# The first norm's modulations on TensorE: a block of two transformers on one Trainium2 core

## What is computed

```python
sh1, sc1, gt1, sh2, sc2, gt2 = [m[:, None, :] for m in adaln_params(c, w_mod[l], b_mod[l])]
csh1, csc1, cgt1, csh2, csc2, cgt2 = adaln_params(c_ctx, w_mod[l], b_mod[l])
pc = project(modulate(ctx, norm1_g[l], csh1, csc1), w_in[l])
...
px = project(modulate(x, norm1_g[l], sh1, sc1), w_in[l])
```

## Time and profile before

| | us |
|---|---|
| median of 3 runs | 1780.99 |
| the profiled execution | 1781.36 |
| its span, first to last instruction | 1779.5 |
| PE busy | 1590.7 (89%) |
| DVE busy | 968.7 (54%) |
| ACT busy | 720.5 (40%) |
| POOL busy | 206.1 (12%) |
| mean granted clock of PE | 0.942 |

### The profile page before, as it was taken

How to read it: one execution, slowest core, us unless ns; L and a number is a source line. 1 busy time by engine, 2 the same in 40 slices (tenths; PEclk the granted TensorE clock), 3 DMA queues, 4 the chain that set the end, 5 groups by cost and what they waited for, 6 DMA issues and landing times.

```text
span 1779.5 us, 18719 instructions
## 1 busy us (share of the span) xinstructions
PE 1590.7 (89%) x7382; PEld 1264.4 (71%) x7382; DVE 968.7 (54%) x1424; ACT 720.5 (40%) x1117; POOL 206.1 (12%) x126
## 2 busy tenths in 40 slices
PE   4597978779899999999989999999787899999995
PEld 2475856547777888888867767787566678888884
DVE  8956656758645333333443655454555666336644
ACT  5324524336633322222233456645345444334431
POOL 4100432325200000000010011120121200000001
PEclk9798989857999999999989999999999999999998
DMA  8374111010022223332322112133212132233221
GB/s 348 117 253 153 48 36 48 24 60 1 1 95 81 97 74 104 107 101 79 105 73 95 59 62 76 53 125 95 71 36 83 48 95 80 94 118 100 80 92 53
DMA packets 47944, 156.57 MB, mean 88 GB/s; under 512 B 5585, under 2 KB 10321, under 8 KB 47345
## 3 DMA queue, kind: packets, MB, share of 16 engines
q1 hardware_dynamic: 42816, 135.29, 23.2%
q10 hardware_dynamic: 5042, 20.09, 3.2%
HBM read 153.26 MB, written 2.10 MB: 87 GB/s over the span
## 4 chain that ended last, share of the span: by engine, by line
PE 73%; DVE 14%; ACT 8%; issue 5%; POOL 1%; DMA 0%; ACTq 0%; DVEq 0%
PE pall L1939 18%; PE pall L1940 18%; PE pall L1941 18%; PE pall L2335 1%; DVE wlo L1157 1%; PE pall L1973 1%; PE pall L1974 1%; PE pall L2337 1%; PE pall L1975 1%; PE pall L2336 1%; PE pall L1957 1%; ACT whi L511 1%; PE pall L1958 1%; PE pall L1959 1%; DVE y L1708 1%
## 5 line engine op out<-in xcount | busy, mean ns | idle before, releaser
L1157 DVE TENSOR_TENSOR wlo<-raw,whi 128x1024 fp32r<-128x1024 f32 (+1 forms) x248 | 271.7, 1096 | 326.8 <-ACT whi L511 326.7
L511 ACT ACTIVATE whi<-raw 128x1024 fp32r<-128x1024 f32 (+2 forms) x263 | 246.4, 939 | 163.8 <-PE pall L1941 121.9
L1939 PE MATMUL pall<-h5h,whi 128*128 128x512 f32 x320 | 125.2, 391 | 1.9 <-DVE wlo L1157 1.9
L1941 PE MATMUL pall<-h5h,wlo 128*128 128x512 f32 x320 | 125.2, 391 | 0.0
L1940 PE MATMUL pall<-h5l,whi 128*128 128x512 f32 x320 | 125.0, 391 | 0.0
L1939 PE MATMUL pall<-h2h,whi 128*128 128x512 f32 x320 | 124.5, 389 | 0.0
L1940 PE MATMUL pall<-h2l,whi 128*128 128x512 f32 x320 | 124.5, 389 | 0.0
L1941 PE MATMUL pall<-h2h,wlo 128*128 128x512 f32 x320 | 124.5, 389 | 0.0
L1939 PE MATMUL pall<-hxh,whi 128*128 128x512 f32 (+1 forms) x136 | 60.4, 444 | 15.3 <-ACT Vd L630 12.3
L1108 ACT ACTIVATE tmp<-pall,vec 128x512 f32<-128x512 f32 x44 | 34.1, 779 | 92.5 <-PE pall L1941 88.2
L1939 PEld LDWEIGHTS pall<-h5h,whi 128*128 128x128 f32 x320 | 60.5, 189 | 15.0 <-issue 2.3
(11 more groups left out here) (424 smaller groups left out, 3839.3 us busy)
## 6 DMA issues: line engine op xcount, KB each, us to landing
raw<-in_weights SPq DMA_DIRECT2D x204, 512.0 KB, 3.4
mraw<-in_wmod ACTq DMA_DIRECT2D x32, 512.0 KB, 5.1
mod<-in_wmod SPq DMA_DIRECT2D x16, 512.0 KB, 11.8
raw<-in_weights SPq DMA_DIRECT2D x25, 256.0 KB, 2.6
raw<-in_weights SPq DMA_DIRECT2D x32, 192.0 KB, 2.3
xT<-in_x SPq DMA_DIRECT2D x1, 2048.0 KB, 19.7
xT<-in_x ACTq DMA_DIRECT2D x1, 2048.0 KB, 8.1
out_y<-xT SPq DMA_DIRECT2D x8, 256.0 KB, 2.1
```

Of the source, the lines that this page charges most:

```text
L511: e.activation(whi[j % 3][:, 0:cols(j)], raw[j % 4][:, 0:cols(j)], ACT.Copy).then_inc(s.hi, 1)
L1157: e.tensor_tensor(wlo[j % 3][:, 0:n], raw[j % 4][:, 0:n], f(whi[j % 3][:, 0:n]), ALU.subtract).then_inc(s.lo_v, 1)
L1939: e.matmul(o_, a[:, kk, :], xh(k), start=(k == 0), stop=False)
L1941: mm = e.matmul(o_, b[:, kk, :], xh(k), start=False, stop=(k == nk - 1))
```

## The change

The 16 modulation blocks of the first norm are made by PE. Their weights now lie untransposed, as 16 units at the end of the `weights` array, in the order `MODS` = 8, 0, 9, 1, 10, 2, ... (scale and shift of feature block 0, then of 1, and so on). PE turns the two conditions into columns (16 products with a slice of `crow` as the weights and a single one as the data), ACT takes their Silu in one instruction of 16 columns (`cols_c`), and each block is 8 products of a [128, 128] weight tile by [128, 2] condition columns, added up in PSUM. `cbx` is still broadcast and made, for the later dot products; `cbc` is not. The dot products, POOL's products and ACT's sums are gone.

The squares are added up by DVE in `acc_c` and `acc`, and PE takes one product with the ones for each of ctx and x, ahead of the tenth and of the fourteenth modulation block.

The bias and the gain are made in two halves (`first_mods`), when 8 and when 16 blocks are done. `hi(0)`, `hi(1)`, `hi(2)` move to after ACT's second, fourth and eighth block of the norm, `lo(0)` to after DVE's third `first_norm`. SP issues `cmT` and `xT` earlier, and weight unit 0 after 13 blocks. The diff, cut to what carries the change:

```diff
+MODS = [8 * j + k for k in range(8) for j in (1, 0)]
...
+    for m in MODS:
+        mt(("mod", m), "w_mod", 128 * m, 8)
     return plan
...
+        cols_c = small[:, 8:24].rearrange("p (k c) -> p k c", c=2)
+        acc_c = work("acc_c", [256], F32, 104)
...
+        def psum_mod(m, n=1):
+            a = bank(7 if m % 8 < 4 else 6, 32).rearrange("p (m c) -> p m c", c=2)
+            return a[:, m:m + n, :]
+
+        def adds(q):
+
+            return 7 * (q // 8) + q % 8
...
-            for m in range(16):
-                if m == 14:
-                    w.wait_ge(s.dot, dot_at[0, 1])
-                if m == 15:
-                    w.wait_ge(s.dot, dot_at[1, 0])
-                    w.wait_ge(s.g_prod, 1)
-                e.dma_start(mod1[m % 14][:, :], ap["wmod"][m]).then_inc(s_m[m % 14], 16)
-                if m == 6:
+            for n in range(16):
+                w.wait_ge(s.mdp, n - 13)
+                j = NU + n
+                src = ap["weights"][offs[j]:offs[j + 1]].rearrange("(p k c) -> p k c", p=128, c=128)
+                e.dma_start(mod1[n][:, :, :], src).then_inc(s_m[n % 14], 16)
+                if n == 5:
                     e.dma_start(cmT[:, :, :], ap["ctx"]).then_inc(s.cm, 16)
-                if m == 12:
+                if n == 8:
                     e.dma_start(xT[:, :, :], ap["x"]).then_inc(s.x, 16)
-            for j in range(4):
+                if n == 12:
+                    load(0)
+            for j in range(1, 4):
                 load(j)
...
-            for i, dst in enumerate((cbx, cbc)):
-                for j in range(2):
-                    w.wait_ge(s.p_cb, 2 * i + j + 1)
-                    e.activation(dst[:, 512 * j:512 * j + 512], bank(2 * i + j), ACT.Silu).then_inc(s.cb, 1)
...
+            w.wait_ge(s.p_cb, 1)
+            e.activation(small[:, 8:24], bank(6, 16), ACT.Silu).then_inc(s.cb, 1)
+            for j in range(2):
+                w.wait_ge(s.p_cb, 2 + j)
+                e.activation(cbx[:, 512 * j:512 * j + 512], bank(2 + j), ACT.Silu).then_inc(s.cb, 1)
+            for q in range(16):
+                n, src, first = (256, cmT, acc_c) if q < 8 else (512, xT, acc)
+                if q % 8 == 0:
+                    w.wait_ge(*((s.cm, 16) if q == 0 else (s.x, 16)))
+                elif q >= 4:
+                    w.wait_ge(s.sqs, adds(q - 4))
+                dst = tmp[q % 4] if q % 8 else first
+                e.activation(dst[:, 0:n], src[:, q % 8, :], ACT.Square).then_inc(s.sq, 1)
             w.wait_ge(s.g_const, 1)
             root("ctx", bank(4, 256), 256, D)
             root("x", bank(5), 512, D)
-            hi(2)
             for i in range(16):
...
+                if i in (1, 3, 7):
+                    hi(i // 3)
...
-            for i, (m, c) in enumerate(DOTS):
-                w.wait_ge(s_m[m % 14], 16 * (m // 14 + 1))
-                w.wait_ge(s.cb, 4 if c else 2)
-                w.wait_ge(s.dot, i - 1)
-                e.tensor_tensor_reduce(junk[i % 2][:, :], mod1[m % 14][:, :], (cbc if c else cbx)[:, :], 1.0, 0.0, ALU.mult,
-                                       ALU.add, accum_out=modv[:, m, c:c + 1]).then_inc(s.dot, 1)
+            for q in range(16):
+                if q % 8:
+                    n, sum_ = (256, acc_c) if q < 8 else (512, acc)
+                    w.wait_ge(s.sq, q + 1)
+                    w.wait_ge(s.sqs, adds(q) - 1)
+                    e.tensor_tensor(sum_[:, 0:n], sum_[:, 0:n], tmp[q % 4][:, 0:n], ALU.add).then_inc(s.sqs, 1)
             newton("ctx", bank(4, 256), 256, D)
             newton("x", bank(5), 512, D)
...
+            def first_mods(k):
+
+                w.wait_ge(s.mdp, 2 * k + 8)
+                w.wait_ge(s.vec, 16)
+                for m in (8 + k, k):
+                    bias = v("b_mod", m, 4).unsqueeze(2).to_broadcast([128, 4, 2])
+                    e.tensor_tensor(modv[:, m:m + 4, :], psum_mod(m, 4), bias, ALU.add).then_inc(s.mdv, 1)
+                w.wait_ge(s.mdv, k // 2 + 2)
+                for c in range(2):
+                    e.scalar_tensor_tensor(gsv[:, c, k:k + 4], modv[:, 8 + k:12 + k, c], 1.0, v("norm1_g", k, 4), ALU.add,
+                                           ALU.mult).then_inc(s.dve, 1)
...
             for i in range(16):
+                if i % 8 == 0:
+                    first_mods(i // 2)
                 first_norm(i)
                 if i:
                     first_rest(i - 1)
+                if i == 2:
+                    lo(0)
             first_rest(15)
+            lo(2)
+            w.wait_ge(s.cb, 3)
...
-            w.wait_ge(s.cb, 4)
-            for i, m in enumerate(pooled):
-                w.wait_ge(s_m[m], 16)
-                w.wait_ge(s.a_prod, i - 1)
-                e.tensor_tensor(prod[i % 2][:, :], mod1[m][:, :], cbc[:, :], ALU.mult).then_inc(s.g_prod, 1)
             lo(1)
             lo(2)
...
-            for i in range(2):
-                for j in range(2):
-                    e.matmul(bank(2 * i + j), ones[0:1, :], crow[0:1, i, 512 * j:512 * j + 512], start=True,
-                             stop=True).then_inc(s.p_cb, 1)
...
+            for k in range(8):
+                for i in range(2):
+                    mm = e.matmul(bank(6, 1, 2 * k + i), crow[0:1, i, 128 * k:128 * k + 128], ones[0:1, 0:1], start=True, stop=True)
+            mm.then_inc(s.p_cb, 1)
+            for j in range(2):
+                e.matmul(bank(2 + j), ones[0:1, :], crow[0:1, 0, 512 * j:512 * j + 512], start=True,
+                         stop=True).then_inc(s.p_cb, 1)
+            w.wait_ge(s.cb, 1)
+            for n, m in enumerate(MODS):
+                if n in (9, 13):
+                    b, size, value, sum_ = (4, 256, 7, acc_c) if n == 9 else (5, 512, 14, acc)
+                    w.wait_ge(s.sqs, value)
+                    e.matmul(bank(b, size), ones[:, :], sum_[:, 0:size], start=True, stop=True).then_inc(s.p_sum, 1)
+                w.wait_ge(s_m[n % 14], 16 * (n // 14 + 1))
+                for k in range(8):
+                    mm = e.matmul(psum_mod(m)[:, 0, :], mod1[n][:, k, :], cols_c[:, k, :], start=(k == 0), stop=(k == 7))
+                mm.then_inc(s.mdp, 1)
```

More of the change, by code:

```diff
@@ L143 @@
     "mt", "mh", "ml", "mlg",
-    "g_const", "p_cb", "cb", "g_prod", "a_prod", "dot", "md", "mod2",
+    "g_const", "p_cb", "cb", "mdp", "mdv", "sqs", "md", "mod2",
     "vg", "dn", "gq", "lam_v", "lam_p", "lam_a",
@@ L185, in build @@
     J = {p[0]: j for j, p in enumerate(plan)}
+    NU = len(plan) - len(MODS)
     job = Order(JOBS)
@@ L261, in build @@
         crow = work("crow", [2, 1024], F32, 88)
-        cbc = work("cbc", [1024], F32, 102)
+        cols_c = small[:, 8:24].rearrange("p (k c) -> p k c", c=2)
+        acc_c = work("acc_c", [256], F32, 104)
         cbx = work("cbx", [1024], F32, 106)
@@ L266, in build @@
         cmT = work("cmT", [8, 256], F32, 48)
-        mod1 = [work(f"mod1_{i}", [1024], F32, a) for i, a in enumerate(list(range(0, 48, 4)) + [56, 60])]
+        mod1 = [work(f"mod1_{i}", [8, 128], F32, a) for i, a in enumerate(list(range(0, 32, 4)) + [56, 60] + list(range(68, 88, 4)) + [96])]
         mraw = [over_x(f"mraw{i}", [1024], 4 * i) for i in range(4)]
-        prod = [work(f"prod{i}", [1024], F32, 72 + 4 * i) for i in range(2)]
-        junk = [work(f"junk{i}", [1024], F32, 80 + 4 * i) for i in range(2)]
         hxh = work("hxh", [8, 512], F32R, 0)
@@ L390, in norm_done @@
             return (s.mlg, mlg_at[name, i]) if (name, i) in by_pool else (s.ml, ml_at[name, i])
-        pooled = [m for m in range(10) if m % 4]
-        DOTS = []
-        for g in range(4):
-            DOTS += [(m, 0) for m in range(4 * g, 4 * g + 4)]
-            DOTS += [(m, 1) for m in range(4 * g, 4 * g + 4) if m not in pooled]
-        dot_at = Order(DOTS)
+        def psum_mod(m, n=1):
[3 more added lines that the diff above has]
+            return 7 * (q // 8) + q % 8
         DOTS2 = {("gv", 2): (0, 3), ("gv", 4): (3, 6), ("gv", 6): (6, 9), ("gd", 0): (9, 12), ("gk", 0, 0): (12, 15),
@@ L487, in _ @@
                 e.dma_start(dst, ap[name]).then_inc(s.const, 16)
-            for j in range(4, len(plan)):
+            for j in range(4, NU):
                 load(j)
@@ L507, in hi @@
             def hi(upto):
-                for j in range(made[0], min(upto + 1, len(plan))):
+                for j in range(made[0], min(upto + 1, NU)):
                     w.wait_ge(s_raw[j % 4], 16 * (j // 4 + 1))
@@ L1015, in _ @@
                     for i in (2 * m - 8, 2 * m - 7):
-                        w.wait_ge(s.p_sq, 14 + i - 1)
+                        w.wait_ge(s.p_sq, i - 1)
                         e.activation(mtile[i % 2][:, :], memT[:, i, :], ACT.Square).then_inc(s.sq, 1)
@@ L1049, in post_square @@
                 w.wait_ge(*x_done(g, k))
-                w.wait_ge(s.p_sq, 21 + 7 * g + k - 3)
+                w.wait_ge(s.p_sq, 7 + 7 * g + k - 3)
                 if k < 4 and k > 0:
@@ L1980, in _ @@
```

(15 more changed lines are left out.)

36 lines of the change are left out of this document (2 added, 34 removed).

## The result

The changed kernel takes **1789.79 us**, the median of 4 runs (1788.91 to 1790.2), beside 1780.83 us (1778.05 to 1781.32) of the kernel before on the same chip: ratio 1.0053, 95% interval 1.0035 to 1.007, a loss of 9.0 us. The profiled execution took 1788.91 us, its span 1787.1.

What follows compares the result with a forecast made beforehand. PE bounds the kernel through its start of gv, the first projection: condition to 13.3, records 54.5, sums 0.85 and 1.7, hand-overs, 71.0 us instead of 62.66. So +8.4 on 1781.36, less 0.37: 1789.4 us, range 1786 to 1795.

Steps and rivals of the forecast that it cites:

- The price of a record: Each thin f32 product on PE is two records, each paced by its weight load: 0.213 us; 256 take 54.5 us.
- The condition, to 13.3 us: PE's start at 3.04 us, condition columns to 9.9 us, then two broadcasts of 3.4 us, ending at 13.3.
- gv's start at 71.0: PE starts gv, the first projection, at 71.0 us instead of 62.66: +8.4 us.
- The choice on which it hung: PE's clock stays at the lower level (1.2 GHz) through the thin products before gv; this case had chance 0.86.
- rival B: Records before gv cost only 0.11 us each; gv at 41.2 us, 21.5 us earlier, total 1760; chance 0.08.
- The norm's chain, 68.4: First norm's steps on ACT and DVE after the sum of x end at 68.4 us, under PE's 71.0.
- x, squares and additions hidden: x lands near 22 us, DVE's squares and additions end near 28, before PE needs them: no cost.
- gv keeps its stretch at the lower level: PE enters gv at the lower clock in both kernels; its 34.7 us stay, give or take one us.
- behind that product ACT empties six banks for 3.1 us with PE idle anyway, which covers the 3 us: After gv, DVE's roughly 3 us lateness for PE's small product is hidden by ACT's 3.1 us emptying.
- +1.5: Upward allowance in the range for waits inside PE's stream and DVE late for the small product after gv.
- C: Rival: load and product don't overlap, a record costs 0.33 us; gv at 105 us, total 1824; chance 0.03.
- D: Rival: clock rises late, at about record 200; gv starts within 3 us of 62.66, no change; chance 0.03 with the like.

Runs made afterwards that it cites:

- e2: Changed kernel with half of the thin records left out (products with k from 4 to 7), executed once: 1769.68 us.
- e11: The changed kernel itself, measured and profiled once more: 1790.48 us.
- e3: Changed kernel, but ACT empties gv's banks before its last modulation loads and DVE makes the lambda product before its dot products: 1792.18 us, ratio 1.0063.
- e4: Changed kernel with PE's two sums ahead of the ninth and tenth modulation block instead of the tenth and fourteenth: 1786.39 us, ratio 1.0032.
- e7: Changed kernel with each thin product widened to 32 columns per load instead of 2, one execution: 1789.98 us.
- e8: The kernel of e3 once more, for its profile, one execution: 1790.93 us.
- e1: Changed kernel with each thin product widened from 2 to 128 columns by a step-0 broadcast, same loads: 1770.39 us, ratio 0.9942.
- e5: Changed kernel with the edits of e1 and e3 together: 1769.84 us, ratio 0.9946.
- e6: e5 with the condition's columns and broadcast brought by DMA instead of made by PE: 1767.9 us, ratio 0.9932.
- e10: e6 with the sum of x two modulation blocks sooner: 1764.29 us, ratio 0.9912.

## Why the prediction was right, and where not

By its own steps:

- **The price of a record, 0.213 us: right.** 144 records took 30.88 us, 0.214 each, all 256 took 54.8 (54.5 foreseen), and e2 halved them in proportion. The sums took 1.20 and 2.06 instead of 0.85 and 1.7, overlapping their neighbours by some 0.2 each.
- **The condition, to 13.3 us: right**, 12.82; the 16 products took 6.98 us (6.8 foreseen). The first starts when the condition lands, at 2.29 to 3.14 us in different executions, and that shifts gv by as much.
- **gv's start at 71.0: 0.2 to 1.0 us too late.** Measured 70.02 in the changed kernel and 70.66 in e11, 70.50 to 70.83 in the profiles of e3, e4, e7 and e8, whose stream is as long. Hand-overs cost next to nothing.
- **The choice on which it hung, that the clock stays low: right, and now for a reason that was tested.** The load time of 333 ns shows the level. PE busy at 100% for 57 us did not bring the rise with 2 columns per load, nor with 32 (e7). With 128 it came after 4.1 us (e1). Two rules of the Trainium skill had spoken for rival B. Its page "TensorE: Matmul & The Clock Gate", section "Why this matters for your kernels", advises keeping TensorE busy. Here the traces disagree with it as a sufficient rule. The page's section "LDWEIGHTS (loading the stationary operand)" puts a load at 107 ns for 128 columns. In these traces loads stand 109 ns apart at the full clock (e1, each 191 ns long) and 213 at the lower one. The figure fits the spacing at the full clock only.
- **The norm's chain, 68.4: right**, `lo(0)` ended at 68.56, and it was off the path: e4 took it 13 us sooner, to 55.72, and gv did not move. The sum of x ended at 60.13 (60.2 foreseen).
- **x, squares and additions hidden: right.** x landed at 22.9, the additions ended at 29.5, and PE waited for no modulation.
- **gv keeps its stretch at the lower level: right, within the one us that the prediction allowed.** The rise came 4.0 us after gv's start (3.8 before) in the first profiles and 6.0 (5.9) in the second ones.
- **The step that failed: "behind that product ACT empties six banks for 3.1 us with PE idle anyway, which covers the 3 us".** I had DVE's lateness right (the norm 10.2 us later, gv 7.4), but took the emptying for work that starts when gv ends. It is behind three loads in ACT's program, which wait for the dot products of the same late DVE. So nothing was covered. The small product waited 2.52 us for DVE (1.01 in e11, where the clock rose later), and between profiles with the same rise the stage grew by 2.8 and 1.3 us. e3 took the wait away, with 34.64 us for the stage (35.40 in e8), and e4 the lateness, with 34.26. The range had +1.5 for it.

That the total came out within 0.4 us of the forecast 1789.4 is in part luck. In the first pair of profiles gv came 1.0 us sooner than forecast and DVE's lateness cost 2.8 more. That would have been a loss of 10.1 us where 8.4 was forecast; +0.6 and +1.2 came in later stages, and -4.4 because the two profiles fell on different times of the attention stages. Up to the end of the attention stages the like pairs give losses of 8.7 and 10.3 us, beside 9.0 and 10.7 by the medians. Rivals B, C and D did not occur. But e1 shows that B's price was to be had: with the operand widened to 128 columns the records came at 0.109 us.

Left open: why the clock takes one course or the other, in gv and through the attention. And what the mending of e3 does far behind gv: the five profiles with it (e3, e5, e6, e8, e10) took 91.9 to 92.6 us in the differential attention, the nine without it 88.8 to 91.2. Next to profiles with the same gated attention that is 1.4 us more at 202 us and 2.6 to 2.9 at 199.4 (e5, e8 and e10 against the changed kernel), about what the mend gained behind gv. DVE's two slowed passes are seen in each of them, but no run separates the two moves of the mend.

## What to carry to other kernels

Before moving sums from an idle engine to TensorE, price each f32 product as two weight loads at the clock that the place will have, and if the operand is thin, widen it with a step-0 broadcast up to the load's own length: that cost nothing here and halved the price. Where a producer gets later, follow it through every queue: an engine that seems free may have a wait of the same producer ahead of the work that you count on as cover. And before a change of 1 to 5 us in an untouched stage is explained, profile both programs twice, and take the engine's waits apart from its work: the work moves with the clock.

## What was unexpected of the hardware

- The same number of loads, all back to back, with the operand 64 times as wide, took 18.29 instead of 30.88 us (144 records), as the clock rose.
- Executions of the kernel before, and of the changed one, differ by 2.3 to 2.6 us in the gated attention and 1.8 in the differential one, without any other engine's work changing; the six runs of e4 lie at 1784.95 to 1785.45 us where the mean granted clock was 0.958 and at 1786.0 to 1787.1 where it was 0.952 to 0.955.
- Ahead of its first recorded change the granted clock reads 1.00 though the loads have the length of the lower level, for 74 us in the changed kernel. The length of a load (333 or 190 ns) tells the level.
- A pass of DVE over 768 columns took 1.02 us when it began 0.19 us ahead of one of POOL, and 1.63 us when POOL's had begun 0.17 us ahead of it; POOL's took 2.23 and 0.98 us.
